# Two sequence mixers: the convolution's group roots taken by tokens on GpSimd and spread by matrix products, and four pieces of work put at other places in the queues

## The chip, the core and the metric

The kernel runs on one core of a Trainium2 chip. A core has a matrix engine (PE, with its weight loads shown apart as PEld), a vector engine (DVE), a scalar engine (ACT), GpSimd (POOL) and a queue that issues transfers (SP). Each engine works through its own list of instructions in order, and semaphores tie the lists together. The metric is the device time of one execution in microseconds (us), and lower is better.

## The reference, cut to what matters

The model runs two layers of a first block (attention, mixture of experts) and then two layers of a second block. A layer of the second block is a feed-forward part, a mixer and a second feed-forward part. Only the mixer of the second block is touched:

```python
h = rms_norm_2(x, mix_norm[l])
rq, rk, rv, rg, mq, mk, mv, ca, cg = split(h @ w_in[l])
y_ret  = silu(rg) * rms(retention(rotary(rq), rotary(rk), rv))    # 6 heads of 64
y_moba = causal_softmax_attention(rotary(mq), rotary(mk), mv)     # 6 heads of 64
u = ca * sigmoid(cg)                                              # 256 channels
y = causal_depthwise_conv(u, 31 taps) + bias
yg = y.reshape(..., 4 groups, 64 channels)
yn = (yg - mean(yg)) * rsqrt(var(yg) + 1e-6)                      # per token and group
y_conv = silu(yn * ln_g + ln_b)
x = x + concat(y_ret, y_moba, y_conv) @ w_out[l]                  # 256 tokens, D = 1024
```

## The kernel before, in words

There are 256 tokens, so two tiles of 128 (`a` is the tile). The mixer is the function `second_mixer`, run once for each of the two layers, and `mix_out` follows it.

**Products.** A large product of float32 values is made of three single-pass products: weights rounded to a high part times the high and the low part of x, and the rest of the weights (low part) times the high part of x. `job` multiplies the 8 column units of `w_in`; a unit is done in two halves of the inner dimension, so there are 16 halves, called by `half(n)` or `job.products(pe, n // 2, n % 2)`. Within a half, the 16 products of the high part for both tiles come first, then the 8 of the low part. ACT rounds the high part of half n (`part_high`, line 599), DVE makes the low part (`part_low`, line 604). In these two mixers the buffers are named the other way round: the tensor `w_lo` holds the high part and `w_hi` the low part. `between` is a call that PE makes after the high products of the last tile, before the low products. `out_job` multiplies by `w_out`: unit 0 and unit 1, each with a first half (inside `second_mixer`) and a second half (in `mix_out`). The first half needs mixed columns 0 to 3, the second columns 4 to 7, which hold the last attention pair and the convolution; `part_mix` (lines 776 and 777, DVE) rounds these columns.

**Start of a mixer.** `rms_columns` turns x into columns: PE transposes (line 471), ACT keeps the high part of 8 chunks (`keep_high`, line 501), DVE makes their low parts (`keep_low`, line 513). Two chunks share one PSUM bank, so ACT waits for DVE before chunks 2, 3, 6 and 7. With `between_low`, DVE makes the low weights of half 0 between chunks 3 and 4. With `between_high`, ACT makes the high weights of half 1 after all 8 chunks. Then ACT squares x for the norm (line 2742).

**Convolution.** DVE adds the 31 taps into `acc` (channels on partitions, two chunks of 256 tokens), in pieces between its other work (line 3193). `conv_means` (PE, bank 7) multiplies by `group_mean`, a 128 by 128 matrix that holds 1/64 inside a group of 64 channels; `centre_conv` (DVE) subtracts; `square_conv` (ACT) squares; `conv_variances` (PE, bank 7) multiplies by `group_mean` again, so every channel holds its group's variance for every token; `root_conv` (ACT, line 3223) takes a square root of 128x512 values; `scale_conv` (DVE, lines 3228 and 3229) inverts and multiplies; `mix_conv` (ACT, line 3235) applies gain, bias and silu. Sqrt, Exp and Silu lie in different tables of ACT; a change of table is an instruction of its own, ACT_TABLE_LOAD.

**Attention.** Six heads in three pairs j. For a pair: `score` (PE, lines 3386 and 3391, banks 4 and 5), `peaks` (DVE), `exponentials` (ACT, line 3407), `invert_sums` (DVE), `normalise` (ACT, line 3418), `turn` (PE transposes, line 3435, banks 6 and 7), `keep_turned` (ACT, lines 3444 and 3445), `sum_values` (PE, line 3456, bank 2), `store` (line 3462). `turn` of head 1 uses bank 7 and so waits for `centre_conv`; `turn` of head 3 waits for `root_conv`.

**Others.** `turn_group(g)` transposes rotated queries and keys (PE, line 3279), and `keep_group(g)` copies them (ACT, line 3287); `score(0)` waits for group 5. `turn_outputs` (PE, line 3362, banks 2 and 3) transposes the retention outputs, and `mix_outputs` (DVE) keeps them. `keep(i)` (ACT, lines 3512 to 3515) keeps projection unit i; `sum_values(0)` needs `keep(7)`. GpSimd has nothing to do in the second half of a mixer. The orders of all engines are written out by hand at the end of `second_mixer`.

Of the kernel before, what the change touches and what calls it, by code (L numbers as in the profile page):

```python
# [24 lines left out]
P = 128  # L25
SEQ = 256
# [262 lines left out]
def build_program(nc, t, out):  # L289
# [272 lines left out]
    class PartedProducts:  # L562
# [46 lines left out]

        def products(self, pe, i, only=None, between=None):  # L610


            width = self.width(i)
            for half in (range(2) if only is None else (only,)):
# [3 lines left out]
                for w_part, x_parts in ((high, (self.x_high, self.x_low)), (low, (self.x_high,))):  # L618
# [8 lines left out]
                    for a in range(TILES):  # L627
# [5 lines left out]
                        for c in range(DC // 2):  # L633
# [3 lines left out]
                            for x_part in x_parts:  # L637
# [3 lines left out]
                                                 stop=cc == DC - 1 and w_part is low)  # L641
                        if w_part is high and a == TILES - 1 and between is not None:
                            between(pe)
# [2106 lines left out]
    def rms_columns(block, next_gains, banks, squares_at=SQUARES_AT, idle=(0, 0, 0), between_high=None,  # L2750
# [19 lines left out]
        @block.scalar  # L2770
        def _(act):
            order = list(x_order)
            if between_high is None:
                square_half(act, *order[0], squares_at), square_half(act, *order[1], squares_at)
                keep_high(act)
                square_half(act, *order[2], squares_at), square_half(act, *order[3], squares_at)
            else:
                keep_high(act)
                between_high(act)
                for a, h in order:  # L2780
                    square_half(act, a, h, squares_at)
# [290 lines left out]
    def second_mixer(block, layer):  # L3072
# [69 lines left out]
        pt_buf = place[:, RET_HEADS * KEYS:RET_HEADS * KEYS + 2 * TILES * SEQ].rearrange("p (h b q) -> p h b q", h=2, b=TILES)  # L3142
        conv_root = place[:, SLOT - 2 * SEQ:].rearrange("p (c q) -> p c q", c=2)
        ret_sums, ret_roots = (stat[:, 64 + 16 * i:64 + 16 * i + TILES * RET_HEADS] for i in range(2))
# [52 lines left out]

        CONV_BANK = 7

        def conv_means(pe):  # L3200
            pe.wait_ge(tapped.sem, tapped.at(2 * KERNEL))
            pe.wait_ge(ret_scaled.sem, ret_scaled.at(1))
            pe.matmul(ps[:, CONV_BANK, :], group_mean, acc.rearrange("p c q -> p (c q)"), start=True,
                      stop=True).then_inc(means.sem, 1)

        def centre_conv(dve):
            dve.wait_ge(means.sem, means.at(1))
            dve.tensor_tensor(acc, acc, ps[:, CONV_BANK, :].rearrange("p (c q) -> p c q", c=2),
                              ALU.subtract).then_inc(centred.sem, 1)
# [5 lines left out]
        def conv_variances(pe):  # L3215
            pe.wait_ge(sq.sem, sq.at(1))
            pe.wait_ge(probs_kept.sem, probs_kept.at(2))
            pe.matmul(ps[:, CONV_BANK, :], group_mean, square.rearrange("p c q -> p (c q)"), start=True,
                      stop=True).then_inc(variances.sem, 1)

        def root_conv(act):
            act.wait_ge(variances.sem, variances.at(1))
            act.activation(conv_root, ps[:, CONV_BANK, :].rearrange("p (c q) -> p c q", c=2), ACT.Sqrt,
                           bias=EPS).then_inc(conv_rooted.sem, 1)

        def scale_conv(dve):
            dve.wait_ge(conv_rooted.sem, conv_rooted.at(1))
            dve_chain.link(dve, dve.reciprocal(conv_root, conv_root))
            dve.tensor_tensor(acc, acc, conv_root, ALU.mult).then_inc(conv_scaled.sem, 1)

# [126 lines left out]
        def turn_outputs(pe):  # L3357

            pe.wait_ge(ret_gated.sem, ret_gated.at(1))
            for c in range(rc):  # L3360
                for a in range(TILES):
# [60 lines left out]
        def turn(pe, j):  # L3422
            for hd in (2 * j, 2 * j + 1):
# [3 lines left out]
                else:  # L3427
                    pe.wait_ge(ret_scaled.sem, ret_scaled.at(1))
                if hd == 1:
                    pe.wait_ge(centred.sem, centred.at(1))  # L3430
                elif hd == 3:
                    pe.wait_ge(conv_rooted.sem, conv_rooted.at(1))
# [34 lines left out]
        def _(pe):  # L3467
# [14 lines left out]
            turn_group(pe, 3), turn_group(pe, 4)  # L3482
            half(13)
            turn_group(pe, 5)
            score(pe, 0)
# [6 lines left out]
            turn(pe, 1)  # L3492
            sum_values(pe, 0)
            score(pe, 2)
            out_job.products(pe, 0, 0)
            sum_values(pe, 1)
            turn(pe, 2)
            out_job.products(pe, 1, 0, between=lambda pe: sum_values(pe, 2))

        @block.scalar  # L3500
        def _(act):
# [46 lines left out]
            square_conv(act)  # L3548
            root_conv(act)
            exponentials(act, 2), exponentials(act, 3)  # L3550
# [11 lines left out]
        def _(dve):  # L3562
# [34 lines left out]
            peaks(dve, 2), peaks(dve, 3)  # L3597
            out_job.part_low(dve, 0, 0)
            invert_sums(dve, 2), invert_sums(dve, 3)
            mix_outputs(dve)  # L3600
# [14 lines left out]
        @block.gpsimd  # L3615
        def _(pool):
            gate_conv(pool)
            root_outputs(pool)
        job.close()
        kept.advance(TILES * len(MIX_UNITS))  # L3620
        for s, n in ((gated, 1), (conv_turned, 1), (conv_kept, 1), (padded, 1), (tapped, 2 * KERNEL), (means, 1), (centred, 1),
                     (sq, 1), (variances, 1), (conv_rooted, 1), (conv_scaled, 1), (conv_mixed, 1), (rotated_ret, TILES),
                     (rotated_moba, 1), (qk_turned, GROUPS), (qk_kept, GROUPS), (ret_scores, RET_HEADS),
# [114 lines left out]
```

## Time and profile before

| | us |
|---|---|
| median of 3 runs | 2247.77 (2246.45 to 2248.02) |
| profiled execution, its own time | 2247.28 |
| its span in the trace | 2245.5 |
| busy in the span: PE, DVE, ACT, POOL | 1953.5, 1071.0, 719.1, 81.2 |

The profile shows start times in us from the start of the span. The first mixer lies at about 1417 to 1546, the second at about 1919 to 2050, and a feed-forward part follows each. Engine queues are read side by side: where one engine's row carries an idle time in brackets, the name behind the arrow is what it waited for. Rows of neighbouring like instructions are merged, with their count behind the x.

### The profile page before, as it was taken

What the parts mean: (1) busy time and instruction counts of PE and PEld (TensorE: products, weight loads), DVE (VectorE), ACT (ScalarE), POOL (GpSimd) and SP (SyncE); (2) the same over time, 40 slices, a digit from 0 to 9 for tenths busy, and PEclk for the clock granted to TensorE, in tenths of its full rate; (3) what the DMA queues carried; (4) which work ended last, traced back from release to release, by engine and by line L of the source; (5) the groups of instructions that cost most, each with busy time, mean ns of one, the idle gap of its engine ahead of it and who ended that gap; (6) DMA issues with size and microseconds to landing.
All of it is one profiled execution on the core that took longest, in us unless ns stands there. A gap on an engine that the chain in (4) does not pass through costs nothing.

```text
span 2245.5 us, 32813 instructions
## 1 busy us (share of the span) xinstructions
PE 1953.5 (87%) x13218; PEld 1370.5 (61%) x13218; DVE 1071.0 (48%) x1609; ACT 719.1 (32%) x1102; POOL 81.2 (4%) x131
## 2 busy tenths in 40 slices
PE   8989667777788986686768999999999999999998
PEld 6755224333365542242423888887888888887887
DVE  4661002011077410020103877787777877777776
ACT  5531002011045210020101443465434443565433
POOL 0000000000011000000000000000000000000000
PEclk9999988988998998888989999999999999999999
DMA  5389999999971899999999655435655656335550
GB/s 199 131 343 419 429 429 423 428 424 428 418 279 43 321 416 428 428 422 429 424 428 397 219 175 190 148 132 173 202 186 170 206 170 209 128 132 178 197 190 25
DMA packets 187949, 624.02 MB, mean 278 GB/s; under 512 B 17654, under 2 KB 129368, under 8 KB 163032
## 3 DMA queue, kind: packets, MB, share of 16 engines
q1 hardware_dynamic: 187864, 622.84, 71.6%
q8 instruction: 59, 0.97, 0.2%
q14 instruction: 26, 0.21, 0.0%
HBM read 621.76 MB, written 1.05 MB: 277 GB/s over the span
## 4 chain that ended last, share of the span: by engine, by line
PE 62%; DMA 28%; DVE 5%; ACT 4%; issue 1%; POOL 0%; DVEq 0%; SPq 0%; POOLq 0%; ACTq 0%
DMA weight_ring<-in_w 27%; PE psum L2945 15%; PE psum L638 12%; PE psum L2917 11%; PE psum L2948 7%; PE psum L2251 4%; PE psum L2229 3%; PE psum L2261 1%; PE psum L2308 1%; PE psum L2403 1%; PE psum L2120 1%; PE psum L2239 0%; DMA arena<-in_p 0%; PE psum L3323 0%; ACT arena L1004 0%
## 5 line engine op out<-in xcount | busy, mean ns | idle before, releaser
L2945 PE MATMUL psum<-x_both,up_hi 128*128 128x512 f32 x1408 | 352.9, 394 | 2.5 <-DVE x_both L513 2.2
L2229 PE MATMUL psum<-weight_ring,arena 128*32 128x256 f32 x3904 | 254.1, 411 | 111.7 <-DMA weight_ring<-in_w 111.7
L2945 PEld LDWEIGHTS psum<-x_both,up_hi 128*128 128x128 f32 x1408 | 257.5, 188 | 57.3 <-issue 3.3
L2229 PEld LDWEIGHTS psum<-weight_ring,arena 128*32 128x32 f32 x3904 | 124.9, 116 | 242.3 <-DMA weight_ring<-in_w 140.0
L2366 DVE TENSOR_TENSOR arena<-arena,psum 128x256 f32<-128x256 f32 x32 | 13.5, 421 | 482.6 <-PE psum L2229 482.6
L2251 PE MATMUL psum<-weight_ring,arena 128*32 128x512 f32 x1024 | 153.1, 731 | 69.7 <-DMA weight_ring<-in_w 60.4
L2997 DVE TENSOR_TENSOR up_lo<-weight_ring,up_hi 128x2048 fp32r<-128x2048 f32 x84 | 192.0, 2286 | 12.2 <-ACT up_hi L2968 11.8
L2948 PEld LDWEIGHTS psum<-x_both,up_lo 128*128 128x128 f32 x1408 | 189.3, 188 | 13.5
L2948 PE MATMUL psum<-x_both,up_lo 128*128 128x256 f32 x1408 | 193.0, 279 | 0.0
L3009 DVE TENSOR_REDUCE arena<-psum 128x256 f32<-128x512 f32 x176 | 121.4, 690 | 129.6 <-PE psum L2948 128.2
L638 PE MATMUL psum<-w_lo,x_both 128*128 128x384 f32 (+3 forms) x768 | 171.2, 360 | 4.7 <-DVE mix_lo L777 2.0
L2968 ACT CAST up_hi<-weight_ring 128x2048 fp32r<-128x2048 f32 x84 | 160.1, 1906 | 15.3 <-PE psum L2948 15.1
L2989 ACT ACTIVATE arena<-arena 128x256 f32<-128x256 f32 x88 | 36.8, 418 | 388.4 <-DVE arena L3015 388.4
L638 PE MATMUL psum<-w_hi,x_both 128*128 128x512 f32 (+3 forms) x640 | 150.6, 367 | 2.8 <-ACT w_hi L599 1.7
L638 PEld LDWEIGHTS psum<-w_lo,x_both 128*128 128x128 f32 x768 | 135.7, 189 | 20.0 <-issue 4.6
L2370 DVE COPY arena<-psum 128x512 f32<-128x512 f32 x30 | 20.7, 691 | 266.6 <-PE psum L2251 266.6
L2261 PE MATMUL psum<-arena 128*128 128x512 f32 x240 | 123.6, 663 | 22.3 <-ACT arena L2326 22.3
L2917 PE MATMUL psum<-down_hi,hid_hi 128*128 128x512 f32 x352 | 138.6, 394 | 0.0
L2917 PE MATMUL psum<-down_hi,hid_lo 128*128 128x512 f32 x352 | 137.8, 392 | 0.0
L2917 PE MATMUL psum<-down_lo,hid_hi 128*128 128x512 f32 x352 | 136.8, 389 | 0.0
L638 PEld LDWEIGHTS psum<-w_hi,x_both 128*128 128x128 f32 x640 | 113.8, 189 | 20.8 <-issue 4.1
L2251 PEld LDWEIGHTS psum<-weight_ring,arena 128*32 128x32 f32 x1024 | 31.7, 122 | 154.5 <-DMA weight_ring<-in_w 75.3
(378 smaller groups left out, 2442.5 us busy)
## 6 DMA issues: line engine op xcount, KB each, us to landing
weight_ring<-in_w SPq DMA_DIRECT2D x186, 2048.0 KB, 25.7
weight_ring<-in_ffn_wg SPq DMA_DIRECT2D x44, 1024.0 KB, 5.9
weight_ring<-in_ffn_wu SPq DMA_DIRECT2D x44, 1024.0 KB, 8.3
weight_ring<-in_ffn_wd SPq DMA_DIRECT2D x44, 1024.0 KB, 4.9
weight_ring<-in_w_in SPq DMA_DIRECT2D x14, 1536.0 KB, 6.8
weight_ring<-in_w_o SPq DMA_DIRECT2D x4, 2048.0 KB, 16.2
arena<-in_w SPq DMA_DIRECT2D x4, 2048.0 KB, 13.9
weight_ring<-in_ple_gate_w SPq DMA_DIRECT2D x4, 2048.0 KB, 25.6
```

The lines of the kernel that those rows point to most:

```text
L638: last = pe.matmul(ps[:, bank, 0:width], x_part[:, cc, a * P:(a + 1) * P], w_part[:, c, :], start=cc == 0 and w_part is high and x_part is ...
L2120: last = pe.matmul(ps[:, ple_banks[i], :], p_cols[:, c, a * P:(a + 1) * P], w[:, c, h * BANK:(h + 1) * BANK], start=c == 0, stop=c == 1)
L2229: last = pe.matmul(ps[j * CAP:(j + 1) * CAP, 4 + k // 2, 0:QW], tokens[:, cc, :], w[c][:, j * QW:(j + 1) * QW], start=cc == 0, stop=cc == ...
L2251: last = pe.matmul(ps[r * CAP:(r + 1) * CAP, 6 + h, :], hc[:, k, r * CAP:(r + 1) * CAP], w[:, r, h, :], start=k == 0, stop=k == 1)
L2261: last = pe.matmul(ps[:, 2 * h + a, :], back[:, a * P:(a + 1) * P], partial[:, h * BANK:(h + 1) * BANK], start=False, stop=False, skip_gro ...
L2917: last = pe.matmul(ps[:, 2 * h + a, :], x_part[:, f, a * P:(a + 1) * P], w_part[:, f, h * BANK:(h + 1) * BANK], start=False, stop=False, s ...
L2945: last = pe.matmul(ps[:, 4 + 2 * f + h, :], w_part[:, f, h, c, :], x_both[:, :, c, :], start=c == 0, stop=False, skip_group_check=True)
L2948: last = pe.matmul(ps[:, 4 + 2 * f + h, 0:SEQ], w_part[:, f, h, c, :], x_hi[:, c, :], start=False, stop=c == DC - 1, skip_group_check=True)
L2968: act.copy(up_hi[:, k % 2], up_weights(k)).then_inc(hi_up.sem, 1)
L2989: act.activation(silu_g[:, k % 2, :], silu_g[:, k % 2, :], ACT.Silu).then_inc(silued.sem, 1)
L2997: dve.tensor_tensor(up_lo[:, k % 2], up_weights(k), up_hi[:, k % 2].bitcast(F32), ALU.subtract).then_inc(lo_up.sem if k % 2 == 0 else used, 1)
L3009: dve.tensor_reduce(joint[:, f, :], ps[:, 4 + 2 * f + h, :].rearrange("p (t q) -> p q t", t=2), AX, ALU.add).then_inc(joined.sem, 1)
```

## The change

The variances are made by tokens: the squares become the stationary operand in 4 products with 2 moving columns (one per group), so bank 7 gets 8 numbers for each of 128 partitions. DVE adds EPS to them (`take_variances`), GpSimd raises them to the power -1/2 (`root_conv`), and PE spreads them back over channels with 8 products of a broadcast column and the identity (`spread_roots`), into bank 3, from which `scale_conv` multiplies. The square root on ACT and the reciprocal on DVE go. The means move from bank 7 to bank 3, so the wait for `centred` moves from `turn` of head 1 to `turn_outputs`. Four calls move: `turn_group(5)` goes inside the second half of unit 6, `sum_values(2)` goes one tile earlier inside `out_job.products(1, 0)`, and at the start of a mixer the high weights of half 1 are made after chunk 3 and not after chunk 7. The wait of `conv_means` for the scaled retention outputs becomes a wait for unit 6 to be kept.

```diff
-        def products(self, pe, i, only=None, between=None):
+        def products(self, pe, i, only=None, between=None, between_tile=TILES - 1):
...
-                        if w_part is high and a == TILES - 1 and between is not None:
+                        if w_part is high and a == between_tile and between is not None:
                             between(pe)
...
             else:
-                keep_high(act)
+                keep_high(act, range(DC // 2))
                 between_high(act)
+                keep_high(act, range(DC // 2, DC))
                 for a, h in order:
                     square_half(act, a, h, squares_at)
...
-        CONV_BANK = 7
+        MEAN_BANK, VARIANCE_BANK, ROOT_BANK = 3, 7, 3
+        group_roots = stat[:, 96:96 + 4 * TILES].rearrange("p (c a g u) -> p c a g u", c=2, a=TILES, u=1)
...
         def conv_variances(pe):
             pe.wait_ge(sq.sem, sq.at(1))
             pe.wait_ge(probs_kept.sem, probs_kept.at(2))
-            pe.matmul(ps[:, CONV_BANK, :], group_mean, square.rearrange("p c q -> p (c q)"), start=True,
-                      stop=True).then_inc(variances.sem, 1)
-
-        def root_conv(act):
-            act.wait_ge(variances.sem, variances.at(1))
-            act.activation(conv_root, ps[:, CONV_BANK, :].rearrange("p (c q) -> p c q", c=2), ACT.Sqrt,
-                           bias=EPS).then_inc(conv_rooted.sem, 1)
+            for c in range(2):
+                for a in range(TILES):
+                    at = (c * TILES + a) * 2
+                    last = pe.matmul(ps[:, VARIANCE_BANK, at:at + 2], square[:, c, a * P:(a + 1) * P],
+                                     group_mean.rearrange("p (g u) -> p g u", g=2)[:, :, 0], start=at == 0,
+                                     stop=at == 4 * TILES - 2, skip_group_check=True)
+            last.then_inc(variances.sem, 1)
+
+        def take_variances(dve):
+            dve.wait_ge(variances.sem, variances.at(1))
+            dve.tensor_scalar(group_roots.rearrange("p c a g u -> p (c a g u)"), ps[:, VARIANCE_BANK, 0:4 * TILES], EPS,
+                              None, ALU.add).then_inc(conv_rooted.sem, 1)
+
+        def root_conv(pool):
+            pool.wait_ge(conv_rooted.sem, conv_rooted.at(1))
+            roots = group_roots.rearrange("p c a g u -> p (c a g u)")
+            pool.tensor_tensor(roots, roots, half_power[:, 0:4 * TILES], ALU.pow).then_inc(conv_rooted.sem, 1)
+
+        def spread_roots(pe):
+            pe.wait_ge(conv_rooted.sem, conv_rooted.at(2))
+            pe.wait_ge(ret_mixed.sem, ret_mixed.at(1))
+            for c in range(2):
+                for a in range(TILES):
+                    for g in range(2):
+                        last = pe.matmul(ps[g * HD:(g + 1) * HD, ROOT_BANK, c * SEQ + a * P:c * SEQ + (a + 1) * P],
+                                         group_roots[:, c, a, g].broadcast_to([P, HD]), ident[:, :],
+                                         start=(c, a) == (0, 0), stop=(c, a) == (1, TILES - 1), skip_group_check=True)
+            last.then_inc(conv_rooted.sem, 1)
...
         def scale_conv(dve):
-            dve.wait_ge(conv_rooted.sem, conv_rooted.at(1))
-            dve_chain.link(dve, dve.reciprocal(conv_root, conv_root))
-            dve.tensor_tensor(acc, acc, conv_root, ALU.mult).then_inc(conv_scaled.sem, 1)
+            dve.wait_ge(conv_rooted.sem, conv_rooted.at(3))
+            dve.tensor_tensor(acc, acc, ps[:, ROOT_BANK, :].rearrange("p (c q) -> p c q", c=2),
+                              ALU.mult).then_inc(conv_scaled.sem, 1)
...
         def turn_outputs(pe):
             pe.wait_ge(ret_gated.sem, ret_gated.at(1))
+            pe.wait_ge(centred.sem, centred.at(1))
...
-                if hd == 1:
-                    pe.wait_ge(centred.sem, centred.at(1))
-                elif hd == 3:
+                if hd == 3:
                     pe.wait_ge(conv_rooted.sem, conv_rooted.at(1))
...
-            half(13)
-            turn_group(pe, 5)
+            job.products(pe, 6, 1, between=lambda pe: turn_group(pe, 5))
...
             sum_values(pe, 0)
+            spread_roots(pe)
             score(pe, 2)
             out_job.products(pe, 0, 0)
             sum_values(pe, 1)
             turn(pe, 2)
-            out_job.products(pe, 1, 0, between=lambda pe: sum_values(pe, 2))
+            out_job.products(pe, 1, 0, between=lambda pe: sum_values(pe, 2), between_tile=0)
...
             square_conv(act)
-            root_conv(act)
...
             out_job.part_low(dve, 0, 0)
+            take_variances(dve)
             invert_sums(dve, 2), invert_sums(dve, 3)
...
             root_outputs(pool)
+            root_conv(pool)
```

## Rows read from the trace of the kernel before

**Rows 1.** The page's chain that ended last, by engine, share of the span.

```profile
PE 62%; DMA 28%; DVE 5%; ACT 4%; issue 1%; POOL 0%; DVEq 0%; SPq 0%; POOLq 0%; ACTq 0%
```

**Rows 2.** Timeline of PE, start of mixer 1: start, duration, engine, line, work, [idle before].

```profile
1423.58 2.04 PE L638 MATMUL psum<-w_hi,x_both 128*128 128x512 f32 x8
1426.39 4.00 PE L638 MATMUL psum<-w_lo,x_both 128*128 128x512 f32 x16 [0.78 <-ACT w_lo L599]
```

**Rows 3.** Timeline of PE, second half of mixer 1.

```profile
1493.36 0.49 PE L3386 MATMUL psum<-weight_ring 64*128 64x128 f32 x4 [0.68 <-ACT weight_ring L3287]
...
1504.27 0.52 PE L3435 MATMUL psum<-ident,arena 128*128 128x128 f32 x3 [0.54 <-DVE arena L3208]
...
1508.05 1.02 PE L3218 MATMUL psum<-arena,chunk_masks 128*128 128x512 f32 x2
...
1513.47 1.59 PE L3435 MATMUL psum<-ident,arena 128*128 128x128 f32 x6 [3.01 <-ACT arena L3418]
1515.15 1.55 PE L3456 MATMUL psum<-weight_ring,arena 128*64 128x256 f32 x8
1516.63 0.52 PE L3386 MATMUL psum<-weight_ring 64*128 64x128 f32 x4
...
1519.37 0.47 PE L638 MATMUL psum<-w_lo,x_both 128*128 128x512 f32 x1 [0.30 <-DVE mix_lo L777]
...
1534.17 0.47 PE L638 MATMUL psum<-w_lo,x_both 128*128 128x512 f32 x1 [0.86 <-DVE mix_lo L777]
```

**Rows 4.** Timeline of PE, mixer 2, two of these places.

```profile
2015.77 1.59 PE L3435 MATMUL psum<-ident,arena 128*128 128x128 f32 x6 [3.01 <-ACT arena L3418]
...
2038.79 0.47 PE L638 MATMUL psum<-w_lo,x_both 128*128 128x512 f32 x1 [0.86 <-DVE mix_lo L777]
```

**Rows 5.** Stretches: length, busy (instructions) of PE, PEld, DVE, ACT, POOL; granted clock; DMA.

```profile
1470.00:1505.00 35.00, 33.66 (x218) 30.74 (x218) 33.23 (x82) 21.74 (x63) 2.98 (x2) 1.00 0.48 156
...
1510.40:1513.40 3.00, 0.07 (x1) 0.00 (x0) 0.80 (x3) 2.99 (x12) 0.00 (x0) 0.99 0.00 0
1513.40:1517.40 4.00, 3.84 (x20) 2.52 (x21) 1.03 (x4) 2.26 (x8) 0.00 (x0) 0.58 0.00 0
...
2015.70:2025.30 9.60, 9.44 (x36) 6.65 (x37) 4.83 (x12) 5.64 (x17) 0.00 (x0) 0.50 0.01 3
```

**Rows 6.** Timeline of ACT, start of mixer 1.

```profile
1419.61 1.60 ACT L501 ACTIVATE x_both<-psum,norm_cols 128x256 fp32r<-128x256 f32 x4 [0.25 <-DVE x_both L513]
1423.68 0.87 ACT L501 ACTIVATE x_both<-psum,norm_cols 128x256 fp32r<-128x256 f32 x2 [2.48 <-DVE x_both L513]
1424.45 1.89 ACT L599 CAST w_lo<-weight_ring 128x2048 fp32r<-128x2048 f32 x1
```

**Rows 7.** Timeline of DVE, start of mixer 1.

```profile
1423.11 0.87 DVE L513 SCALAR_TENSOR_TENSOR x_both<-psum,norm_cols,x_both 128x256 fp32r<-128x256 f32 x2
```

**Rows 8.** Timeline of ACT, second half of mixer 1.

```profile
1506.21 0.65 ACT L3213 ACTIVATE arena<-arena 128x512 f32<-128x512 f32 x1
1506.88 1.28 ACT L3223 ACT_TABLE_LOAD   x1
...
1509.73 1.28 ACT L3407 ACT_TABLE_LOAD   x1
...
1514.00 1.05 ACT L3515 ACTIVATE arena<-psum,stat 128x384 f32<-128x384 f32 x2
```

**Rows 9.** Timeline of PE, four two-pass products of a broadcast column and the identity.

```profile
1553.20 0.60 PE L2898 MATMUL psum<-ident,stat 128*128 128x128 f32 x4
```

**Rows 10.** Groups of GpSimd in mixer 1: busy, mean ns, idle before.

```profile
L721 POOL TENSOR_TENSOR stat<-stat,half_power 128x12 f32<-128x12 f32 x1 | 2.4, 2400 | 0.1
...
L721 POOL TENSOR_TENSOR stat<-stat,half_power 128x2 f32<-128x2 f32 x1 | 0.7, 723 | 0.1
```

**Rows 11.** Timeline of DVE, second half of mixer 1.

```profile
1517.99 1.23 DVE L777 TENSOR_TENSOR mix_lo<-mix_cols,x_both 128x1024 fp32r<-128x1024 f32 x1
...
1522.92 3.33 DVE L3228 RECIPROCAL weight_ring<-weight_ring 128x512 f32<-128x512 f32 x1
```

More of the change, by code:

```diff
@@ L3142, in second_mixer @@
         pt_buf = place[:, RET_HEADS * KEYS:RET_HEADS * KEYS + 2 * TILES * SEQ].rearrange("p (h b q) -> p h b q", h=2, b=TILES)
-        conv_root = place[:, SLOT - 2 * SEQ:].rearrange("p (c q) -> p c q", c=2)
         ret_sums, ret_roots = (stat[:, 64 + 16 * i:64 + 16 * i + TILES * RET_HEADS] for i in range(2))
@@ L3195, in add_taps @@
                     last.then_inc(tapped.sem, 1)
-        CONV_BANK = 7
+        MEAN_BANK, VARIANCE_BANK, ROOT_BANK = 3, 7, 3
+        group_roots = stat[:, 96:96 + 4 * TILES].rearrange("p (c a g u) -> p c a g u", c=2, a=TILES, u=1)
         def conv_means(pe):
             pe.wait_ge(tapped.sem, tapped.at(2 * KERNEL))
-            pe.wait_ge(ret_scaled.sem, ret_scaled.at(1))
-            pe.matmul(ps[:, CONV_BANK, :], group_mean, acc.rearrange("p c q -> p (c q)"), start=True,
+            pe.wait_ge(kept.sem, kept.at(7 * TILES))
+            pe.matmul(ps[:, MEAN_BANK, :], group_mean, acc.rearrange("p c q -> p (c q)"), start=True,
                       stop=True).then_inc(means.sem, 1)
@@ L3207, in centre_conv @@
             dve.wait_ge(means.sem, means.at(1))
-            dve.tensor_tensor(acc, acc, ps[:, CONV_BANK, :].rearrange("p (c q) -> p c q", c=2),
+            dve.tensor_tensor(acc, acc, ps[:, MEAN_BANK, :].rearrange("p (c q) -> p c q", c=2),
                               ALU.subtract).then_inc(centred.sem, 1)
@@ L3621, in second_mixer @@
         for s, n in ((gated, 1), (conv_turned, 1), (conv_kept, 1), (padded, 1), (tapped, 2 * KERNEL), (means, 1), (centred, 1),
-                     (sq, 1), (variances, 1), (conv_rooted, 1), (conv_scaled, 1), (conv_mixed, 1), (rotated_ret, TILES),
+                     (sq, 1), (variances, 1), (conv_rooted, 3), (conv_scaled, 1), (conv_mixed, 1), (rotated_ret, TILES),
                      (rotated_moba, 1), (qk_turned, GROUPS), (qk_kept, GROUPS), (ret_scores, RET_HEADS),
```

## The prediction, as put on record

> **What bounds the kernel now.** I read the page's chain first, then the timelines of PE, ACT and DVE side by side over the first mixer, then the same places in the second, and last the granted clock by stretches. Over the whole span the chain is PE 62% and DMA 28% [rows 1]. DMA belongs to the first block. In the mixers no transfer ends a wait, so what counts there is where PE stands idle and what each idle stretch waits for.
>
> The idle stretches of mixer 1 are these. At its start PE waits 0.78 us for ACT to round the high weights of half 1 [rows 2]. In the second half it waits 0.68 us for the copy of transposed group 5, 0.54 us for the centred convolution, 3.01 us for normalised probabilities, 0.30 and 0.86 us for rounded mixed columns [rows 3]. Mixer 2 has the same waits, and it is 2.3 us slower: the place that stands at 1534.17 in mixer 1 [rows 3] stands at 2038.79 in mixer 2 [rows 4], 504.62 later, while the turn that ends the long wait stands only 502.30 apart, at 1513.47 [rows 3] and 2015.77 [rows 4].
>
> The 2.3 us are a matter of PE's clock. It runs at 1.00 (2.4 GHz) over 1470 to 1505, though 1.3 us of that are idle in pieces under 1 us. After the 3.01 us wait it falls to 1.2 GHz: mean 0.58 over 1513.4 to 1517.4 in mixer 1, and 0.50 over all of 2015.7 to 2025.3 in mixer 2 [rows 5]. So the long wait costs twice, once as idle time and once in slow products behind it.
>
> **Start of a mixer.** ACT keeps chunks 2 to 5 from 1419.61 to 1421.21, waits 2.48 us for DVE, keeps chunks 6 and 7, and only then rounds the weights, 1424.45 to 1426.34 [rows 6]. With the rounding (1.89 us) after chunk 3 it starts at about 1420.4 and ends at 1422.3, inside ACT's idle time. Chunks 4 and 5 are then kept at 1422.3 to 1423.1. DVE takes chunk 4 at 1423.11 [rows 7], because its own low weights come first, so it finds chunk 4 (kept 1422.7) and chunk 5 ready, with about 0.4 us to spare, and chunks 6 and 7 stay where they were. Nothing else is queued behind on ACT but four squarings, which end 1.9 us earlier than before. PE goes on at once after its 8 low products (end 1425.6 [rows 2]). Gain: 0.78 us per mixer.
>
> **Group 5.** Its transposes go ahead of the last 8 low products of unit 6, so ACT can copy it 0.5 us earlier, and the 0.68 us wait mostly goes. What is late next is DVE: it is busy 33.23 of the 35 us up to 1505 [rows 5] with taps and low weights, and nothing here shortens them. The exponentials of pair 0 wait for DVE's peaks and `conv_means` for DVE's last tap. I give this edit 0.2 us at `conv_means`, within 0 and 0.6.
>
> **Means in bank 3.** `turn` of head 1 no longer waits for the centring, which cost 0.54 us [rows 3]; it then waits for its probabilities until about 1503.7. Centring (end 1503.95) is done when `turn_outputs` comes. With the edit above, PE is 0.5 us earlier from `turn_outputs` on, so the high products of half 15, which ended at 1508.05 [rows 3], end at about 1507.5.
>
> **The square root leaves ACT.** Before: squares end at 1506.86, a table load begins at 1506.88, the root waits for the variances and runs, a second load of 1.28 begins at 1509.73, so the exponentials of pair 1 begin at 1511.0 [rows 8]. After: squares end at 1506.86 (ACT's own work ahead of them sets that), the peaks of pair 1 are there since about 1505.5, and the exponentials begin at 1506.9. Gain on ACT: 4.1 us, of which 2.56 are two table loads. The Trainium skill ("ScalarE: Activation LUTs", "What ACT_TABLE_LOAD costs") adds a drain of about 1380 ns to each load; by it two loads would be worth 5.3 us. The trace has no such gap: the first load starts 0.02 us after the squares [rows 8], so the sum goes by 1.28.
>
> What is late next: variances. PE makes the variances in 8 instructions (4 products, each two passes). The nearest row is four such instructions in 0.60 us, the last lasting 0.27, so 0.11 each [rows 9]: 0.9 us, about what the two wide ones took (1.02 with their tail [rows 3]). If 2 moving columns cost less than 128, it may be half of that. They end at 1508.45. DVE adds EPS (0.2), then inverts the sums of heads 2 and 3, whose exponentials end at 1508.6. ACT normalises from 1508.95 to 1510.45, then keeps unit 7 in 1.05 us [rows 8], ending at 1511.5. PE ended half 15 at 1510.46 (1513.47 less 3.01 [rows 3]) and now ends it at 1509.95, turns heads 2 and 3 between 1510.0 and 1510.9 and needs unit 7: `sum_values(0)` begins at 1511.5 rather than 1515.15 [rows 3]. Gain: 3.6 us.
>
> **Clock at that place.** The idle stretch shrinks from 3.01 us to some 0.3 and 0.6 us with six transposes between. In 1470 to 1505 pieces of this size left the clock at 1.00 [rows 5], so I take full clock. `sum_values(0)` took 1.48 us at 1.2 GHz (1515.15 to 1516.63 [rows 3]) and so takes about 0.8. It ends at 1512.3.
>
> **The roots come back.** GpSimd's power took 2.40 us on 12 columns and 0.72 on 2 [rows 10], so 8 columns are about 1.7 us. It starts at about 1509.0 and ends at 1510.8, 1.5 us before PE asks. The 2.40 was measured beside a busy DVE, so contention is in it. `spread_roots` is 16 instructions at 0.11 [rows 9], 1.7 us, wholly on PE's path; with half as many stationary columns it may be 1.0, and at the full 0.19 of a weight load 3.0. `score(2)` begins at 1514.1 rather than 1516.63 and takes 2.44. DVE's mixed columns, 1.23 us for the last step [rows 11] and 2.7 us in all after `sum_values(0)`, are ready at 1515.1, so that 0.30 us wait goes too. First half of unit 0: 1516.5 rather than 1519.37 [rows 3]. Gain so far 2.8 us.
>
> **End of the mixer.** From 1519.37 to 1534.17 there were 13.9 us of work and 0.86 of waiting. The last attention pair is now summed one tile (1.85 us) earlier, ending at 1526.9. ACT: the last turned head is copied by 1525.5, table load 1.28 and silu 1.1 end at 1527.9. DVE rounds the columns in 2.0 us, ready at 1530.0, and PE is free at 1530.5. The wait of 0.86 goes with half a microsecond to spare. The reciprocal, 3.33 us on DVE [rows 11], lay behind PE's products: if it had stayed, `mix_conv` would still have found its input in time. `mix_out` begins at 1530.5 rather than 1534.17: 3.7 us.
>
> **Sum.** Mixer 1: 0.78 + 3.7 = 4.5. Mixer 2: the same, and the 2.3 us of slow clock that mixer 1 did not have: 6.8. Together 11.2 us (4.48 + 6.8, rounded down), of the profiled execution's own 2247.28: **2236.0 us**. That execution stands 0.5 below the median of the runs shown, within their spread. Behind a mixer PE sets the pace and all of it passes to the end. SP gets its two spare ring slots back about 4 us earlier too, so no transfer becomes late.
>
> **Rivals.**
> 1. The clock still falls. For it: the stretch 1507.5 to 1516.5 becomes thin, with 2-column products, transposes, 64-column products and about 1 us idle. Against: 1470 to 1505 has the like at 1.00. Price where it falls as in mixer 2: spread +1.4, sums +0.7, scores +1.4, first products +1.0, so 4.4 us. In one mixer: 2240.4. In both: 2244.8, within the noise.
> 2. A dearer spread: 3.0 us in place of 1.7 gives 2238.6.
> 3. The start gains nothing (DVE late on chunks 4 to 7): 2237.6.
> 4. Slower: the clock falls and stays at 1.2 GHz over the first half of unit 0 as well. 24 products of 128x512 at 0.23 us each (8 in 2.04 with a tail of 0.4 [rows 2]; (2.04 - 0.4) / 7) then cost twice that, 5.5 us more, less the 1.0 already counted. Both mixers: 2244.8 + 9.0 = 2253.8. To end above 2252.3 by it takes some 8 us of gain lost per mixer, so about 17 us at low clock behind `turn`; mixer 2 before had 9.6 us in all [rows 5].
>
> **Chances.** Full clock, with 2 and 3 as variants: 0.74. The clock falls in one mixer: 0.13. In both: 0.09. Rival 4: 0.04. What a measurement of this kernel can tell from no change is about 0.2%, 4.5 us. So below 2243.3: 0.86; within: 0.09; slower: 0.05. The range runs from 2232 (spread at 1.0, group 5 worth its 0.6, variances nearly free) to 2243, which takes in a dear spread and one fallen clock.
>
> **What the profile would show.** No idle time at the second product batch near 1426; no ACT_TABLE_LOAD between the squares and the exponentials; PE's largest wait in the mixer under 1 us; a clock of 1.00 throughout both mixers; 16 spread products in 1.7 us; a POOL power of 1.7 us that nobody waits for; feed-forward parts of unchanged length. The prediction is wrong if PE waits on POOL, if the clock falls behind the turns, or if DVE's taps turn out to set the pace up to half 15.

## The result, and the profile after

The changed kernel takes 2231.26 us (median of 4 runs, 2229.82 to 2232.07), the kernel before 2247.11 (4 runs, 2245.84 to 2248.02). The ratio of their runs is 0.993, 95% interval 0.9918 to 0.9942, or 15.9 us less by the medians. Forecast were 2236.0 us and a range of 2232 to 2243. The direction was right. The forecast gain was 11.3 us and 15.9 came, and the time lies 0.7 us below the range.

PE's timeline of the changed kernel gives the mixer piece by piece (columns as before; lines 3460, 3481, 3412 and 3388 are the turns, the values, the scores and `turn_outputs`, 3224 and 3246 the new variances and spread):

```profile
1415.76 1.91 PE L471 MATMUL psum<-ident,x 128*128 128x128 f32 x16
...
1418.25 4.06 PE L638 MATMUL psum<-w_lo,x_both 128*128 128x512 f32 x16 [0.58 <-DVE x_both L513]
...
1424.02 3.91 PE L638 MATMUL psum<-w_lo,x_both 128*128 128x512 f32 x16
...
1492.43 3.02 PE L638 MATMUL psum<-w_lo,x_both 128*128 128x384 f32 x16
...
1497.52 0.49 PE L3412 MATMUL psum<-weight_ring 64*128 64x128 f32 x4 [0.68 <-ACT arena L3433]
...
1502.26 3.02 PE L638 MATMUL psum<-w_lo,x_both 128*128 128x384 f32 x16
1505.12 0.95 PE L3224 MATMUL psum<-chunk_masks,arena 128*128 128x2 f32 x8
...
1507.41 1.07 PE L3460 MATMUL psum<-ident,arena 128*128 128x128 f32 x6
1508.91 0.87 PE L3481 MATMUL psum<-weight_ring,arena 128*64 128x256 f32 x8 [0.43 <-ACT arena L3540]
1509.58 1.07 PE L3246 MATMUL psum<-ident,stat 128*64 128x128 f32 x16
1510.58 0.49 PE L3412 MATMUL psum<-weight_ring 64*128 64x128 f32 x4
...
1512.74 0.48 PE L638 MATMUL psum<-w_lo,x_both 128*128 128x512 f32 x1
...
1537.64 1.91 PE L471 MATMUL psum<-ident,x 128*128 128x128 f32 x16
```

The first and the last of these rows are the same place in two parts of the kernel: the first transpose of a mixer and the first transpose of the feed-forward part behind it. Their distance is the length of a mixer, 121.88 us here. It leaves out everything upstream, and where the clock stays up it is the same in both mixers to 0.03 us, so all runs below are compared by it. The same two rows of the kernel before are 128.18 us apart. Between them stands its wait at the start of the mixer:

```profile
1417.17 1.91 PE L471 MATMUL psum<-ident,x 128*128 128x128 f32 x16
...
1419.66 4.08 PE L638 MATMUL psum<-w_lo,x_both 128*128 128x512 f32 x16 [0.58 <-DVE x_both L513]
...
1545.35 1.91 PE L471 MATMUL psum<-ident,x 128*128 128x128 f32 x16
```

The long wait of 3.01 us [rows 3] is gone. What is left are waits of 0.68 and 0.43 us, and another of 0.58 at the start that was there before. The clock stays at 1.00 over both mixers, also where it had fallen [rows 5]. In these two windows, the granted clock is the third number from the end:

```profile
1507.00:1511.00 4.00, 3.54 (x38) 2.68 (x36) 2.10 (x4) 2.94 (x10) 0.99 (x1) 1.00 0.02 4
...
2003.00:2007.00 4.00, 3.54 (x39) 2.68 (x37) 2.13 (x4) 2.94 (x10) 0.97 (x1) 1.00 0.01 4
```

On ACT the exponentials (line 3433) follow the squares directly, with no table load between, where [rows 8] have two. GpSimd takes the power of 8 columns in 1.64 us:

```profile
1503.74 0.65 ACT L3215 ACTIVATE arena<-arena 128x512 f32<-128x512 f32 x1
1504.27 0.38 ACT L3433 ACTIVATE arena<-psum,arena 128x128 f32<-128x128 f32 x1
```

```profile
1506.35 1.64 POOL L3237 TENSOR_TENSOR stat<-stat,half_power 128x8 f32<-128x8 f32 x1 [20.09 <-DVE stat L3231]
```

The profiled spans are 2245.5 and 2229.1 us, 16.4 apart. Lengths by the transposes:

| | mixer 1 | two feed-forward parts | mixer 2 | start of mixer 1 |
|---|---|---|---|---|
| before | 128.18 | 187.00, 187.12 | 130.50 | 1417.17 |
| changed | 121.88 | 186.97, 187.10 | 121.91 | 1415.76 |

The two mixers give 6.30 + 8.59 = 14.9 us, the feed-forward parts nothing. The other 1.4 us stand ahead of mixer 1, where no line was changed.

### The profile page after: what moved, and what is told of

Read it like the earlier page. It is cut to its first block, busy times and chain, and to the rows that moved or that the text cites. A ratio compares the mean times of both kernels' runs of the same rounds, so it can differ in the third digit from the quotient of the medians.

```text
span 2229.1 us, 32885 instructions
## 1 busy us (share of the span) xinstructions
PE 1942.8 (87%) x13244; PEld 1367.7 (61%) x13262; DVE 1064.9 (48%) x1609; ACT 712.9 (32%) x1096; POOL 84.6 (4%) x133
## 4 chain that ended last, share of the span: by engine, by line
PE 61%; DMA 27%; DVE 6%; ACT 3%; issue 1%; SPq 1%; POOL 1%; DVEq 0%; POOLq 0%; ACTq 0%
DMA weight_ring<-in_w 25%; PE psum L2946 15%; PE psum L638 11%; PE psum L2918 11%; PE psum L2949 7%; PE psum L2251 4%; PE psum L2229 4%; PE psum L2261 2%; DVE arena L3193 1%; PE psum L2308 1%; DMA weight_ring<-in_ple_gate_w 1%; SPq L181 1%; PE psum L2403 1%; PE psum L2120 1%; DVE w_hi L604 1%
## 5 line engine op out<-in xcount | busy, mean ns | idle before, releaser
L2229 PE MATMUL psum<-weight_ring,arena 128*32 128x256 f32 x3904 | 263.0, 422 | 111.0 <-DMA weight_ring<-in_w 110.8
L2251 PE MATMUL psum<-weight_ring,arena 128*32 128x512 f32 x1024 | 147.3, 705 | 72.5 <-DMA weight_ring<-in_w 63.1
L2261 PE MATMUL psum<-arena 128*128 128x512 f32 x240 | 118.5, 639 | 22.2 <-ACT arena L2326 22.2
```

The lines of the kernel that those rows point to most:

```text
L2229: last = pe.matmul(ps[j * CAP:(j + 1) * CAP, 4 + k // 2, 0:QW], tokens[:, cc, :], w[c][:, j * QW:(j + 1) * QW], start=cc == 0, stop=cc == ...
L2251: last = pe.matmul(ps[r * CAP:(r + 1) * CAP, 6 + h, :], hc[:, k, r * CAP:(r + 1) * CAP], w[:, r, h, :], start=k == 0, stop=k == 1)
L2261: last = pe.matmul(ps[:, 2 * h + a, :], back[:, a * P:(a + 1) * P], partial[:, h * BANK:(h + 1) * BANK], start=False, stop=False, skip_gro ...
```

## The experiments

Every variant was made from the kernel before or the changed one. Its mixer lengths and the time at low clock (from windows of half a microsecond) are in one table at the end of this section.

**moves_only.** The new way to the roots undone (the edit in words, not in code):

```diff
 # from the changed kernel
-    4 narrow variance products, take_variances, power on GpSimd, spread_roots
+    wide variance product in bank 7, square root on ACT, reciprocal on DVE
```

> The four moves and the means in bank 3, with the square root on ACT and the reciprocal on DVE as before. Length of a mixer (first transpose at its start to first transpose of the feed-forward part behind it): before 128.18 and 130.50 us, changed kernel 121.88 and 121.91. Theory A (the root's way is worth most, and the clock falls as long as the wait for pair 1's probabilities stays near 3 us): mixers of about 125.5 and 127, clock still 1.2 GHz for some us behind that wait, whole kernel 5 to 6 us faster than before. Theory B (the moves hold most of the gain): mixers of 123 or less, 10 us or more faster.

2242.15 us (8 runs, 2237.4 to 2244.91), ratio 0.9973 (0.9962 to 0.9983), 5.3 us less than the runs of before beside it (2247.48). The mixers are 127.74 and 127.43, longer than either theory said; the whole-kernel figure is theory A's. The profile shows the longest of the eight executions (2244.91 us, the shortest is 2237.4), so these mixers may be longer than those of the median run. PE waits as long as ever for pair 1, since ACT's chain to the root moves up together with PE (its wait for the variances is 0.48 us where it was 0.95):

```profile
1513.14 1.58 PE L3438 MATMUL psum<-ident,arena 128*128 128x128 f32 x6 [3.02 <-ACT arena L3422]
```

The clock falls behind that wait, in mixer 1 for 10.2 us, where the profile of before has 3.4:

```profile
1512.50:1522.50 10.00, 9.27 (x36) 6.55 (x37) 5.22 (x13) 6.05 (x16) 0.00 (x0) 0.51 0.01 2
1522.50:1530.00 7.50, 7.50 (x41) 5.80 (x40) 5.91 (x5) 4.24 (x14) 0.00 (x0) 1.00 0.00 0
2017.00:2024.00 7.00, 7.00 (x30) 5.05 (x27) 4.34 (x10) 3.98 (x12) 0.00 (x0) 0.52 0.01 4
```

**roots_only.** The moves undone, with the waits that go with bank 7 (not shown) put back as before:

```diff
 # from the changed kernel
-                keep_high(act, range(DC // 2))
+                keep_high(act)
                 between_high(act)
-                keep_high(act, range(DC // 2, DC))
...
-        MEAN_BANK, VARIANCE_BANK, ROOT_BANK = 3, 7, 3
+        MEAN_BANK, VARIANCE_BANK, ROOT_BANK = 7, 7, 3
...
-            job.products(pe, 6, 1, between=lambda pe: turn_group(pe, 5))
+            half(13)
+            turn_group(pe, 5)
...
-            out_job.products(pe, 1, 0, between=lambda pe: sum_values(pe, 2), between_tile=0)
+            out_job.products(pe, 1, 0, between=lambda pe: sum_values(pe, 2))
```

> The roots by tokens on GpSimd, spread by products; the four moves undone, means in bank 7. Theory A: exponentials of pair 1 right behind the squares, clock 1.00 in both mixers, mixers of about 124.5 each, 9 to 10 us faster than before. Theory B: the waits that the moves removed come back larger, mixers above 126, less than 6 us faster.

2236.65 us (5 runs, 2235.44 to 2240.03), ratio 0.9957 (0.9943 to 0.9971), mixers 124.52 and 124.52, no low clock. By mixers that is theory A; beside 128.18 and 130.50 it is 9.6 us, and 10.8 by the medians.

**cast_only.** The kernel before with the rounding after chunk 3.

```diff
-                keep_high(act)
+                keep_high(act, range(DC // 2))
                 between_high(act)
+                keep_high(act, range(DC // 2, DC))
```

> The kernel before with one edit: high weights of half 1 after chunk 3. Two theories of how a wait is to be priced. Theory A (by the bracketed idle time of the row): half 1 starts 0.78 us earlier, counted from the first transpose. Theory B (the row's idle time leaves out the modelled tail of the last product, so start to start counts): 0.96 us earlier (9.22 to 8.26).

Half 1 begins 8.27 us after the first transpose, against 9.22 before: 0.95 us, theory B.

```profile
1414.64 1.91 PE L471 MATMUL psum<-ident,x 128*128 128x128 f32 x16
...
1422.91 3.44 PE L638 MATMUL psum<-w_lo,x_both 128*128 128x512 f32 x14
```

Yet mixer 1 comes out at 129.38, longer than before: its clock stayed low for 10.2 us, not 3.4.

**filler.** The kernel before with the long wait filled:

```diff
         def turn(pe, j):
+            if j == 1:
+                pe.wait_ge(probs_kept.sem, probs_kept.at(1))
+                for _ in range(13):
+                    pe.matmul(ps[:, 6, :], zeros_bf[:, 0:P], zeros_bf[:, :], start=True, stop=True)
             for hd in (2 * j, 2 * j + 1):
```

> The kernel before with 13 products of zeros (128x512, bf16, about 0.22 us each at 2.4 GHz, into bank 6, which is free there) put on PE ahead of the turn that waits 3.01 us; no result depends on them. Theory A (the slow clock comes from that idle stretch alone, and idle time and clock are separate prices): clock 1.00 in both mixers, both mixers 127.5 us long, a saving of about 0.7 and 3.0 us against the profiled run of before, 3 to 5 us in the medians. Theory B (the narrow work behind the stretch lets the clock fall anyway): the clock still falls, mixers as before.

2243.22 us (10 runs, 2239.91 to 2245.97), ratio 0.9988 (0.9978 to 0.9997). Both mixers are 127.52 us and the clock is 1.00 throughout: theory A to a few hundredths. PE's work behind the wait starts when it did before (96.32 us after the first transpose, before 96.30), so the filler delays nothing, and 127.52 is the mixer of before without its clock losses. The profile of before lost 0.66 and 2.98 us to the clock. In the medians the filler saves 3.0 us beside the runs of before (2246.20), at the lower end of theory A, with 0.7 to 4.9 as the interval. The trace has a record of 12 of the 13 products:

```profile
1508.47 2.75 PE L3426 MATMUL psum<-zeros_bf 128*128 128x512 bf16 x12
1511.42 1.23 PE L3439 MATMUL psum<-ident,arena 128*128 128x128 f32 x6 [0.19 <-ACT arena L3418]
```

**tables.** Only the table loads brought back:

```diff
             square_conv(act)
+            act.activation(stat[:, 110:111], stat[:, 109:110], ACT.Sqrt)
```

> The changed kernel with a square root of one column on ACT behind the squares, which nothing reads: it brings the two table loads back and nothing else. Theory A (a load costs its row, 1.28 us, so about 2.9 with the tiny root): exponentials of pair 1 begin 2.9 us later, the values of pair 0 are summed 2.9 us later, and PE gets an idle stretch of about 2.6 us. Theory B (1.28 plus a drain of 1.38 each): 5.6 us later. The clock: if it needs the full 3 us stretch to fall it stays 1.00 and the mixers are 124.8 us long; if not, they are longer by 0.7 to 3.

```profile
1505.51 0.65 ACT L3215 ACTIVATE arena<-arena 128x512 f32<-128x512 f32 x1
1506.18 1.28 ACT L3574 ACT_TABLE_LOAD   x1
1507.47 0.20 ACT L3574 ACTIVATE stat<-stat 128x1 f32<-128x1 f32 x1
1507.68 1.28 ACT L3433 ACT_TABLE_LOAD   x1
1508.98 0.37 ACT L3433 ACTIVATE arena<-psum,arena 128x128 f32<-128x128 f32 x1
```

From the start of the squares to the exponentials it is 3.47 us instead of 0.53, so 2.9: theory A, each load costs its 1.28 and no drain beside it. The rest of theory A was too high: the values of pair 0 are summed 95.61 us after the first transpose where the changed kernel has 93.15, so 2.46 us later and not 2.9, since in the changed kernel ACT had waited 0.38 us for DVE just behind the exponentials. PE's wait is 2.09 us, shorter than the 2.6 expected, and the clock falls all the same, in both mixers:

```profile
1511.43 1.59 PE L3460 MATMUL psum<-ident,arena 128*128 128x128 f32 x6 [2.09 <-ACT arena L3444]
1513.11 1.55 PE L3481 MATMUL psum<-weight_ring,arena 128*64 128x256 f32 x8
```

```profile
1505.00:1509.00 4.00, 4.00 (x27) 4.00 (x27) 2.25 (x2) 3.95 (x9) 0.88 (x1) 1.00 0.00 0
1511.50:1515.00 3.50, 3.41 (x23) 2.53 (x25) 0.64 (x2) 1.76 (x5) 0.00 (x0) 0.54 0.02 5
```

The mixers are 125.09 and 125.91, 3.2 and 4.0 us longer than in the changed kernel. Of this 2.46 is the wait, and the remaining 0.75 and 1.54 are the clock.

**spread_twice.** The three loops of `spread_roots` run twice.

```diff
+            for turn_ in range(2):
-            for c in range(2):
+                for c in range(2):
```

> The changed kernel with the 16 spreading instructions issued twice. Theory A (an instruction with 64 stationary columns costs 0.06 us start to start, all on PE's path): 1.0 us longer per mixer, 122.9. Theory B (0.11 each, as with 128 stationary columns): 1.7 us longer. Theory C (hidden behind DVE's mixed columns): no longer.

```profile
1508.33 1.95 PE L3247 MATMUL psum<-ident,stat 128*64 128x128 f32 x32
1510.21 0.49 PE L3413 MATMUL psum<-weight_ring 64*128 64x128 f32 x4
```

From the first of these rows to the second, 32 instructions take 1.88 us, 0.059 each, and the mixers are 122.77 and 122.76, 0.9 us longer. Theory A.

**no_tile, no_group5.** One move of the changed kernel undone in each.

```diff
 # no_tile
-            out_job.products(pe, 1, 0, between=lambda pe: sum_values(pe, 2), between_tile=0)
+            out_job.products(pe, 1, 0, between=lambda pe: sum_values(pe, 2))
 # no_group5
-            job.products(pe, 6, 1, between=lambda pe: turn_group(pe, 5))
+            half(13)
+            turn_group(pe, 5)
```

> The changed kernel with the last pair's values summed after the second tile again. Theory A (DVE's rounding of columns 4 to 7 ends last there): the wait for mixed columns comes back, start to start about 1.1 us (0.86 in brackets), mixers 123.0. Theory B (with the reciprocal gone DVE is early enough either way): mixers 121.9.

> The changed kernel with group 5 turned after unit 6 again. Theory A (DVE's peaks and taps are late next and swallow it): mixers no more than 0.2 us longer, 122.1. Theory B (start to start, the wait of 0.68 was 0.96 and all of it counts): 0.9 us longer, 122.8.

Without the tile's move the bracket of 0.86 is back, and the mixers are 122.98, 1.10 us longer: theory A, and again more than the bracket. The row of no_tile:

```profile
1527.70 0.47 PE L638 MATMUL psum<-w_lo,x_both 128*128 128x512 f32 x1 [0.86 <-DVE mix_lo L777]
```

Without group 5's move they are 122.05 and 122.04, 0.17 us longer: theory A. Its own wait is 0.68 again, but the next one, for the exponentials, shrinks from 0.68 to 0.20. Counted from the first transpose, the scores of pair 0 start 0.63 us later than in the changed kernel and those of pair 1 only 0.16, so three quarters of this edit's gain is lost again at the next wait.

```profile
1492.38 0.49 PE L3412 MATMUL psum<-weight_ring 64*128 64x128 f32 x4 [0.68 <-ACT weight_ring L3312]
...
1499.16 0.49 PE L3412 MATMUL psum<-weight_ring 64*128 64x128 f32 x4 [0.20 <-ACT arena L3433]
```

**pow_three.** Two more powers on GpSimd ahead of the one that counts.

```diff
+            for _ in range(2):
+                pool_chain.link(pool, pool.tensor_tensor(stat[:, 104:112], roots, half_power[:, 0:4 * TILES], ALU.pow))
             pool.tensor_tensor(roots, roots, half_power[:, 0:4 * TILES], ALU.pow).then_inc(conv_rooted.sem, 1)
```

> The changed kernel with GpSimd's power taken three times (the first two into a place that nobody reads). The power ends 1.6 us before PE asks, and one lasts 1.64 us. Theory A (GpSimd hides with a slack of about 1.6 us): 3.3 us more on GpSimd make PE wait about 1.7 us before spreading, mixers of 123.6 us less what the wait for mixed columns gives back; the clock stays 1.00. Theory B (the spread is not on the path): mixers 121.9.

```profile
1509.19 1.09 PE L3248 MATMUL psum<-ident,stat 128*64 128x128 f32 x16 [1.69 <-POOL stat L3239]
```

PE waits 1.69 us and the mixers are 123.81 and 123.82, 1.9 longer. Theory A, with nothing given back later. This wait did not lower the clock.

**taps_early, taps_early_means.** The changed kernel with DVE's taps in earlier gaps, and then with the means ahead of the scores of pair 1.

```diff
-            add_taps(dve, 0, 3)
+            add_taps(dve, 0, 5)
             part(5)
...
             part(14)
-            add_taps(dve, 21, 27)
+            add_taps(dve, 27, KERNEL)
             part(15)
             peaks(dve, 0), peaks(dve, 1)
-            add_taps(dve, 27, KERNEL)
...
 # taps_early_means, besides
-            score(pe, 1)
             conv_means(pe)
+            score(pe, 1)
```

> The changed kernel with DVE's taps earlier: 5, 3, 3, 2, 2, 1, 1, 2, 2, 2, 4, 4 taps at the places of before, so that the last taps stand ahead of the low part of half 15 and fill DVE's waits before 1475. Theory A (DVE's queue sets the pace of pair 0's probabilities and of the means): exponentials of pair 0 about 0.3 us earlier, their normalising 2 us earlier, half 15 about 0.5 us earlier, mixers of 121.2 us or less, 1.5 us or more off the whole. Theory B (what PE waits for is ACT's own chain): mixers 121.6 to 121.9, no difference to the changed kernel that a median shows.

> As taps_early, with the means made ahead of the second pair's scores, in PE's wait for the exponentials (0.68 us in brackets, about 0.9 start to start; the means take 0.87). Theory A: another 0.4 to 0.6 us per mixer off. Theory B (ACT's normalising of pair 1 ends last anyway): same as taps_early.

taps_early: 2230.02 us (5 runs, 2228.0 to 2230.96), ratio to before 0.9924 (0.9911 to 0.9938), mixers 121.53 and 121.56. That is 0.35 per mixer, between the theories: PE's wait for the exponentials is 0.32 instead of 0.68, and ACT now starts them right behind its own table load, with no wait for DVE. taps_early_means: 2228.85 us (5 runs, 2227.12 to 2230.02), ratio 0.992 (0.9907 to 0.9934), mixers 120.73 and 120.74, another 0.8 each, more than theory A said. Only two waits of PE are left in its mixer 1:

```profile
1418.50 4.07 PE L638 MATMUL psum<-w_lo,x_both 128*128 128x512 f32 x16 [0.58 <-DVE x_both L513]
...
1508.00 0.87 PE L3481 MATMUL psum<-weight_ring,arena 128*64 128x256 f32 x8 [0.43 <-ACT arena L3540]
```

By the mixers it beats the changed kernel by 2.3 us. The medians differ by 2.4, on different chips.

All lengths, and the time at 1.2 GHz:

| | mixer 1 | mixer 2 | low clock, us | start of mixer 1 |
|---|---|---|---|---|
| before | 128.18 | 130.50 | 3.4, 10.2 | 1417.17 |
| filler | 127.52 | 127.52 | 0, 0 | 1415.10 |
| cast_only | 129.38 | 128.59 | 10.2, 6.8 | 1414.64 |
| moves_only | 127.74 | 127.43 | 10.2, 6.8 | 1418.33 |
| roots_only | 124.52 | 124.52 | 0, 0 | 1414.96 |
| tables | 125.09 | 125.91 | 3.4, 3.4 | 1417.50 |
| pow_three | 123.81 | 123.82 | 0, 0 | 1413.46 |
| no_tile | 122.98 | 122.98 | 0, 0 | 1415.91 |
| spread_twice | 122.77 | 122.76 | 0, 0 | 1414.51 |
| no_group5 | 122.05 | 122.04 | 0, 0 | 1417.24 |
| changed | 121.88 | 121.91 | 0, 0 | 1415.76 |
| taps_early | 121.53 | 121.56 | 0, 0 | 1415.79 |
| taps_early_means | 120.73 | 120.74 | 0, 0 | 1416.01 |

## Why the prediction was wrong in size and right in kind

**Where the gain lies.** Between the two profiles the mixers give 14.9 us. Clock: 0.66 + 2.98 = 3.6, shown by filler for these two profiles (3.0 in the medians). The new way to the roots, at full clock: 127.52 to 124.52, 3.0 per mixer, shown by roots_only. The moves on top of it: 124.52 to 121.9, 2.6 per mixer, of which the last pair's values are 1.10 and group 5 is 0.17. The rounding after chunk 3 gave 0.95 in cast_only. The remaining 0.4 are the means in bank 3 with the wait that changed along with them. No run has this edit alone, but two traces bracket it: up to half 15, roots_only and no_group5 differ by it and by the rounding. Half 15 starts 88.05 us after the first transpose in the one (first row) and 86.66 in the other (second row), 1.39 earlier. The rounding has 0.95 of this, which leaves 0.44.

```profile
1503.01 3.02 PE L638 MATMUL psum<-w_lo,x_both 128*128 128x384 f32 x16
```

```profile
1503.90 3.02 PE L638 MATMUL psum<-w_lo,x_both 128*128 128x384 f32 x16
```

Within the new way to the roots the two table loads weigh most: tables puts them back into the changed kernel with a root of one column, and 2.46 us are lost again, clock aside, of the 3.0.

**The clock's term held.** The sum had 2.3 us for mixer 2 and the halving of `sum_values(0)`, 0.68, in each mixer: 3.7 in all, measured 3.6. Rival 1 and rival 4, a clock that falls again, did not come. The reason given, that waits under 1 us leave it at 1.00, held in every run. The close match owes something to luck, since sum and measurement stand on the same profiled execution of before, and the clock's cost differs from one execution to the next (last section). But the room was smaller than I took it to be: tables shows a fall after a single bracket of 2.09 us, while 1.69 in pow_three did not do it.

**The sum without the clock was too small**, 7.6 us where 11.2 came. The steps that failed are mis-sized terms:

1. *"`spread_roots` is 16 instructions at 0.11, 1.7 us."* They took 1.00 (1509.58 to 1510.58), 0.06 each. The row that I scaled had 128 stationary columns, the new product has 64. I had the low end of 1.0 and chose the other one. Worth 1.4 us over both mixers; spread_twice shows the rate a second time.
2. *Each wait was priced by its bracket.* The bracket starts at the modelled end of the last product, not where the next product could have started. Start to start, the wait of 0.78 was worth 0.95 (cast_only), that of 0.86 was worth 1.10 (no_tile), and 1.69 was worth 1.93 (pow_three). The same error made `score(2)` 2.44 us long; it takes 2.16 (1510.58 to 1512.74), so the wait behind it [rows 3] was 0.58 and not 0.30. Over the rounding, that wait and the last one this is 0.17 + 0.28 + 0.24 = 0.7 per mixer, 1.4 in all.
3. The rest, some 0.7 to 0.8 us, is spread thinly. Per mixer, `sum_values(0)` lasts 0.67 and not 0.8. Half 15 starts 86.50 us after the first transpose against 88.02 before, a gain of 1.52 where the sum had 1.28; 0.17 of the difference is the rounding of step 2, so 0.07 are new. Another 0.16 come between half 15 and `sum_values(0)`. The cause of these small ones is open.

**A reading that was not quite right.** The prediction says that mixer 2 of the kernel before has the same waits as mixer 1. The wait of 0.30 us for mixed columns is missing there: PE is still slow at that place and reaches it at 2022.84, after DVE is done (2021.5). The 2.3 us between the mixers are thus what is left of the slow clock once that wait is taken off. The sum does not change by it, since it used the whole lengths.

**Right, step by step.** From the start of the squares to the exponentials it was 4.8 us before (1506.21 to 1509.73 and the load of 1.28 [rows 8]) and is 0.53 now, 4.3 earlier where 4.1 was forecast. The power on GpSimd was forecast at 1.7 and took 1.64; its slack of about 1.6 us is confirmed by pow_three. `sum_values(0)` is 4.83 us earlier than before, forecast 4.4. Group 5 was forecast at 0.2 and is worth 0.17, for the reason given: what came next was late too. That also answers the last sign of being wrong, DVE's taps: moving them gains 0.35 us per mixer (taps_early), so they do hold PE back before half 15, but as the prediction had it, as the next thing that is late, and by little. The variances, forecast at 0.9, took 0.80. The Trainium skill's drain of about 1380 ns ("ScalarE: Activation LUTs", "What ACT_TABLE_LOAD costs") is not seen at either load of tables. There the first load starts 0.02 us after the squares end and the exponentials start 0.02 us after the second load ends, so the sum was right to leave the drain out. Rival 2 (a dear spread) and rival 3 (no gain at the start) are refuted by spread_twice and cast_only.

**The range.** Its low end stood on the low spread, a full group 5 and nearly free variances, and had nothing for brackets that run short. It had nothing either for what lies outside the change: the profiles put the start of mixer 1 anywhere from 1413.46 to 1418.33 us with the same code ahead of it. The changed kernel's profile stands 1.4 us to the good side of the one before. The mixers' 14.9 alone would give 2247.28 - 14.9 = 2232.4, just inside the range, so it is within this scatter that the time fell 0.7 us below the low end. The 3.6 us by which the forecast was too careful in the mixers are no scatter. With 1.4 of that scatter and the mixers' 14.9, the difference of the spans is accounted for.

## What to carry to other kernels

Price a wait by start to start times of the products around it, not by the bracketed idle time: here each bracket on PE was 0.17 to 0.28 us short. Measure each change inside a stretch between two like instructions, since scatter elsewhere (5 us here) is larger than most edits. And where a long wait precedes dense work on PE, count its clock as a term of its own and as a draw, not a constant: here it was worth 0.7 to 3 us per mixer beside the idle time, at its largest as much as the new way to the roots (3.0).

## What the hardware showed beyond what was expected

A single wait of about 3 us cost the same idle time in every run but a different amount of slow clock: 3.4, 6.8 or 10.2 us at 1.2 GHz behind it (before, cast_only and moves_only, six mixers). The two mixers of before, the same code in one profile, differ by 2.3 us at this place, and an edit that saves 0.95 us can come with a longer mixer. A wait of 2.09 us in the bracket (tables) brought 3.4 us of low clock in both mixers, and the same 3.4 us cost 0.75 us in the one and 1.54 in the other: in mixer 1 the low clock begins with the short transposes and the pause behind them, in mixer 2 only at 2013.0, with the spread and the scores.

Two-pass float32 products of a broadcast column and the identity follow one another every 0.06 us with 64 stationary columns, and those with 128 every 0.11 [rows 9]. Products with 128 stationary and only 2 moving columns take 0.10 each (0.80 for 8), so fewer moving columns bought almost nothing.
